# A two-part network on one core: the first part's second feed-forward product by seven block products instead of eight

## The reference

```python
x = x + jnp.concatenate([ya, yb, yc], axis=-1) @ w_out
u = _rms(x, norm2) @ w_ff1
return x + jnp.square(jax.nn.relu(u)) @ w_ff2
```

## Time and profile before

| | |
|---|---|
| runs | 2923.84, 2929.8, 2934.4 us; median 2929.8 us |
| span of the profiled execution | 2923.6 us |
| its TensorE clock granted, mean | 0.969 |
| PE busy | 2783.6 us (95%) |
| DVE busy | 1440.3 us (49%) |
| ACT busy | 988.4 us (34%) |
| POOL busy | 170.2 us (6%) |
| HBM read | 211.83 MB, 73 GB/s over the span |

### The profile page before, as it was taken

How to read it: one execution, slowest core, us unless ns; L and a number is a source line. 1 busy time by engine, 2 the same in 40 slices (tenths; PEclk the granted TensorE clock), 3 DMA queues, 4 the chain that set the end, 5 groups by cost and what they waited for, 6 DMA issues and landing times.

```text
span 2923.6 us, 45193 instructions
## 1 busy us (share of the span) xinstructions
PE 2783.6 (95%) x20028; PEld 2299.7 (79%) x20028; DVE 1440.3 (49%) x2242; ACT 988.4 (34%) x1490; POOL 170.2 (6%) x166
## 2 busy tenths in 40 slices
PE   8989999999989999999999799999999897999998
PEld 7877888878768888887768778888887587788887
DVE  4575533344475444433454574343634645743436
ACT  4344322233344232323342233232333522332422
POOL 0200000001100000000013300000000033000000
PEclk9998999999989999999989899999999898999999
DMA  5102222223003222221000033222220001132221
GB/s 192 50 1 97 87 101 96 92 73 114 17 8 136 94 94 101 93 92 52 15 1 30 20 128 115 90 102 90 85 73 29 1 3 46 73 130 101 87 101 58
DMA packets 31011, 216.83 MB, mean 74 GB/s; under 512 B 3680, under 2 KB 3936, under 8 KB 6368
## 3 DMA queue, kind: packets, MB, share of 16 engines
q1 hardware_dynamic: 30816, 213.94, 20.2%
HBM read 211.83 MB, written 2.10 MB: 73 GB/s over the span
## 4 chain that ended last, share of the span: by engine, by line
PE 88%; DVE 8%; ACT 2%; issue 1%; PEld 0%; PEldq 0%; DMA 0%; ACTq 0%; SPq 0%; DVEq 0%
PE PS L570 81%; PE PS L573 3%; PE PS L771 2%; DVE SC L1381 2%; DVE X L1389 1%; DVE R L1381 1%; DVE SM L1392 1%; PE PS L1185 1%; PE PS L1135 1%; DVE LN L1381 0%; PE PS L855 0%; DVE SM L1381 0%; ACT LN L2172 0%; PE PS L764 0%; PEld PS L570 0%
## 5 line engine op out<-in xcount | busy, mean ns | idle before, releaser
L570 PE MATMUL PS<-H,SPL 128*128 128x512 f32 (+1 forms) x4560 | 1054.2, 391 | 5.5 <-DVE H L1389 4.0
L570 PEld LDWEIGHTS PS<-H,SPL 128*128 128x128 f32 (+1 forms) x4560 | 851.5, 188 | 188.5 <-issue 7.0
L1381 DVE TENSOR_TENSOR SPL<-RAW,SPL 128x2048 fp32r<-128x2048 f32 (+3 forms) x192 | 429.6, 2239 | 680.5 <-ACT SPL L2172 677.5
L2172 ACT ACTIVATE SPL<-RAW 128x2048 fp32r<-128x2048 f32 (+3 forms) x192 | 358.0, 1868 | 783.0 <-PE PS L570 754.8
L570 PE MATMUL PS<-SPL,Uu 128*128 128x512 f32 x2592 | 589.8, 389 | 0.0
L570 PEld LDWEIGHTS PS<-SPL,Uu 128*128 128x128 f32 x2592 | 486.5, 188 | 101.0
L570 PE MATMUL PS<-SPL,H 128*128 128x512 f32 (+2 forms) x2016 | 432.1, 375 | 2.3 <-DVE SPL L1381 1.6
L570 PEld LDWEIGHTS PS<-SPL,H 128*128 128x128 f32 x2016 | 363.7, 189 | 69.2 <-DVE SPL L1381 2.1
L2172 ACT ACTIVATE R<-PS 128x512 f32<-128x512 f32 (+1 forms) x154 | 88.5, 584 | 187.0 <-PE PS L570 156.3
L1381 DVE TENSOR_TENSOR R<-R,PS 128x512 f32<-128x512 f32 (+1 forms) x98 | 64.8, 661 | 106.6 <-PE PS L570 91.2
L2172 ACT ACTIVATE Uu<-R 128x512 fp32r<-128x512 f32 x108 | 68.3, 632 | 142.2 <-DVE R L1381 142.2
(11 more groups left out here) (240 smaller groups left out, 2481.7 us busy)
## 6 DMA issues: line engine op xcount, KB each, us to landing
RAW<-in_wA SPq DMA_DIRECT2D x84, 1024.0 KB, 4.8
RAW<-in_wB SPq DMA_DIRECT2D x84, 1024.0 KB, 4.8
RAW<-in_wAo SPq DMA_DIRECT2D x8, 1024.0 KB, 4.8
RAW<-in_wBo SPq DMA_DIRECT2D x8, 1024.0 KB, 5.0
LN<-in_ln SPq DMA_DIRECT2D x4, 1024.0 KB, 6.6
P<-in_pB SPq DMA_DIRECT2D x2, 1920.0 KB, 9.1
RAW<-in_wBm SPq DMA_DIRECT2D x4, 704.0 KB, 4.0
X<-in_x SPq DMA_DIRECT2D x4, 512.0 KB, 5.6
```

The source lines that it names most:

```text
L570: return pe.matmul(out, l_, r_, start=start, stop=stop)
L1381: return v.tensor_tensor(out, a, b, o)
L2172: return a.activation(out, in_, f, scale=scale)
```

## The change

In the first-kind layers (`QUADS` has the parts 0 to 3 for the layers 0 and 1, and none for 2 and 3) the down product of each part is made by seven products of blocks in place of eight. The matrix of hidden values (512 tokens x 1024) is cut into A11, A12, A21, A22 (256 tokens x 512), the weights (1024 x 1024) into B11, B12, B21, B22 (512 x 512, each one group of the stream). The products are

- P1 = A11·B11, P2 = A12·B21, P5 = S1·T1, P3 = S4·B22, P6 = S2·T2, P7 = S3·T3, P4 = A22·T4, in this order;
- the sums of weights T1 = B11 + B12, T2 = T1 + B22, T3 = B12 + B22, T4 = B21 + T2;
- the sums of hidden values S3 = A11 - A21, S1 = A21 - A22, S2 = -A22 - S3, S4 = A12 + S2, by VectorE (`row_sum`).

Each has 24 multiplies (2 tiles of 128 tokens x 4 blocks x 3). P6 and P7 go on in the banks 0 and 1 of P1, P3 goes on in the banks 4 and 5 of P5; a product that goes on in a bank first waits until VectorE has added what stands there to x. The 16 additions to x have the numbers of `xadd`.

The weight sums are made by transfers that GpSimd issues, which add what they read to what lies in SBUF (`accum_op`). T3 is made as soon as its block is loaded; T1, T2 and T4 are a chain, since T1 and T2 lie where B11 lay, and each sum waits until the low part of what lay there before is made. Raw weights now have four places (`RAW`, `RW2`, and `LN`), and a group's place and what frees it come from `load_plan`.

The root of the norm can no longer be applied behind the product, since blocks of tokens are mixed; TensorE spreads the roots over the partitions once a layer (`spread_roots`, between the first two groups of the first up product), ScalarE copies them to `RB`, and VectorE makes relu(u)·root from PSUM, which ScalarE squares in place.

```diff
-GROUPS_A, GROUPS_B = 47, 50
+LOADS_A, LOADS_B = 47, 50
+QUADS = ((0, 1, 2, 3), (0, 1, 2, 3), (), ())
...
+            def spread_roots(l):
+
+                pe.wait_ge(s.nr, 8 * (l + 1))
+                bank_free(4)
+                for t in range(4):
+                    ins = mm(bank(4)[:, t * 128:(t + 1) * 128], rms[t][:, 1:2].to_broadcast([128, 128]), C("ident"))
+                ins.then_inc(s.gtr, 1)
+                free[4] = (s.rc, l + 1)
+
+            def quad(key):
+
+                base, ready = n["xadd"], n.get("ul", 0)
+                added_to = {("P6", 0): 1, ("P6", 1): 2, ("P3", 0): 5, ("P3", 1): 6, ("P7", 0): 9, ("P7", 1): 10}
+                for name in PRODUCTS:
...
+                    pe.wait_ge(s.lo, i + 1)
+                    pe.wait_ge(s.ul, ready + lows)
+                    goes_on = (name, 0) in added_to
+                    for b in range(2):
+                        if goes_on:
+                            pe.wait_ge(s.xadd, base + added_to[name, b])
+                        else:
+                            bank_free(PBANKS[name][b])
...
+                low_operand("A12", slice(2, 4))
+                row_sum("S1")
+                low_parts()
+                low_operand("S1")
+                add("P1", 0, 0, 0, True)
+                add("P1", 1, 1, 0, True)
+
+                row_sum("S2")
+                add("P2", 0, 0, 0)
+                low_operand("S2")
+                row_sum("S4")
+                low_parts()
+                add("P2", 1, 1, 0)
+
+                low_operand("S4")
+                add("P5", 0, 2, 1, True)
+                low_parts()
+                add("P5", 1, 3, 1, True)
+
+                add("P3", 0, 0, 1, True)
+                low_parts()
+                add("P3", 1, 1, 1, True)
+
+                low_operand("A22")
+                low_parts()
+                add("P6", 0, 0, 1, op=ALU.subtract)
+                ended(0)
+                add("P6", 1, 1, 1, op=ALU.subtract)
+                ended(1)
+
+                low_parts()
+                add("P7", 0, 2, 0, True)
+                add("P7", 0, 2, 1, op=ALU.subtract)
+                add("P7", 1, 3, 0, True)
+                add("P7", 1, 3, 1, op=ALU.subtract)
+
+                low_parts()
+                add("P4", 0, 2, 0)
+                ended(2)
+                add("P4", 1, 3, 0)
+                ended(3)
...
+                    def squared(q, b):
+                        v.wait_ge(s.mm, full_at[(l, "up", p, q), b])
+                        stt(RU[q][:, b], bank(sets[q][b]), 0.0, RB, ALU.max, ALU.mult).then_inc(s.fv, 1)
...
+                g.wait_ge(s.raw[held["B12"]], landed["B12"])
+                g.dma_start(B12, block("B22"), accum_op=ALU.add).then_inc(s.tx, 16)
+                g.wait_ge(s.lo, j + 1)
+                g.dma_start(B11, block("B12"), accum_op=ALU.add).then_inc(s.ty, 16)
+                g.wait_ge(s.lo, j + 3)
+                g.dma_start(B11, block("B22"), accum_op=ALU.add).then_inc(s.ty, 16)
+                g.wait_ge(s.lo, j + 2)
+                g.wait_ge(s.ty, summed["T2"][1])
+                g.dma_start(B21, B11, accum_op=ALU.add).then_inc(s.ty, 16)
...
-                if i >= 2:
-                    sp.wait_ge(s.lo, i - 1)
-                sp.dma_start(raw(i), src).then_inc(s.raw[i % 2], 16)
+                if freed is not None:
+                    sp.wait_ge(s.lo, freed)
+                sp.dma_start(raw_slots[where][:, 0:w], src).then_inc(s.raw[where], 16)
```

More of the change, by code:

```diff
@@ L142, in weight_stream, with split_widths @@
     return stream
-def first_group(l):
-    return l * GROUPS_A if l < 2 else 2 * GROUPS_A + (l - 2) * GROUPS_B
+def split_widths(stream):
+    widths = []
+    loads, splits, quads = load_plan()
+    at = 0
+    for l in range(4):
+        k = first_load(l)
+        for _ in range(INPUTS[l] + 4):
+            widths.append(stream[k][1])
+            k += 1
+        for p, n_up in enumerate(N_UP[l]):
+            for _ in range(n_up):
+                widths.append(stream[k][1])
+                k += 1
+            widths += [2048] * 7 if p in QUADS[l] else [stream[k + i][1] for i in range(N_DOWN)]
+            k += N_DOWN
+    return widths
 def split_plan():
@@ L1321, in tensor @@
                     for q in range(2):
[L1322 to L1329, removed]
+                        chunk((l, "up", p, q), 2, of_h2, "F", sets[q], freed=lambda b: (s.fv, n("fv")),
+                              between=(lambda: spread_roots(l)) if p == q == 0 else None)
+                    quad((l, "down", p))
             for l in range(2):
@@ L1440, in chunk, with paid, low_operand @@
                             evict(b)
+            def paid():
+                while at["owed"]:
+                    at["owed"] -= 1
+                    low_parts()
+            def low_operand(which, ks=slice(0, 4)):
+                i, a_ = OPERANDS[which]
+                hi, lo = operand(i)
+                v.wait_ge(s.uh, n("uh"))
+                ins = tt(four(lo)[:, ks], a_[:, ks], four(hi)[:, ks].bitcast(f32), ALU.subtract)
+                if ks.stop == 4:
+                    ins.then_inc(s.ul, 1)
+                    n("ul")
@@ L2191, in high_part @@
             def high_part(j):
-                w = stream[j][1]
-                a.wait_ge(s.raw[j % 2], 16 * (j // 2 + 1))
+                w = widths[j]
+                where, landed, summed = splits[j]
+                if summed is None:
+                    a.wait_ge(s.raw[where], landed)
+                else:
+                    chained, value = summed
+                    a.wait_ge(s.ty if chained else s.tx, value)
                 if slot_prev[j] is not None:
@@ L2732, in scalar @@
                         logs()
[L2733 removed]
+                    if four_sums:
+                        a.wait_ge(s.fbv, 22 * l + 8 * p + 8)
+                        quad((2 + l, "down", p))
+                    else:
+                        dense("ln" if p == 2 else None)
         def gpsimd(g):
@@ L2910, in sync @@
             sp.dma_start(PSM[:, 0:NPS], ap["psm"]).then_inc(s.psm, 16)
-            for i, (src, w) in enumerate(stream):
+            for i, (l_, k_, where, freed) in enumerate(loads):
+                src, w = stream[first_load(l_) + k_]
                 if i == 3:
```

386 lines of the change are left out of this document (329 added, 57 removed).

## The result

The changed kernel takes 2936.7 us (median of 20 runs, 2926.1 to 2948.2) where the kernel before takes 2924.5 (20 runs, 2913.1 to 2936.9): a ratio of 1.0042, 95% interval 1.0029 to 1.0055. It is slower by 0.4%; 0.5% faster was forecast.

What follows compares the result with a forecast made beforehand. TensorE, busy 95% of the span, was taken as the bound. Roots 2.1 and layer end 2.9 lost, down products 19.5 gained: -14.5, so 2929.8 - 14.5 = 2915.3 us, range 2908 to 2956.

Steps and rivals of the forecast that it cites:

- The weight sums: Step on GpSimd's adding transfers in the down products: the chain T2, T4 lands in time and costs nothing.
- D: Time from issue to landing of a GpSimd transfer that adds: put at 7.6 us, free up to 7.85.
- c: Delay of T4's landing when a plain load shares the transfer engines: 2.8 us.
- latest landing that costs nothing: T4's limit, 25.1 us after a down product's first multiply, when ScalarE's part of its split must start for P7.
- My own case: Weight sums with D at 7.6 us, inside the limit by 0.25, costing nothing; D up to 8.2 had chance 0.43.
- the bounds of D: For the adding transfer: from below a plain load's 4.8 us, from above two loads in a row, 9.6.
- P3's wait: In each down product TensorE waits for VectorE's additions of P5: 2.8 us, then another 0.2, together 3.0.
- three signs of being wrong: D over 8.75 us, TensorE waiting for anything in the up products, or the granted clock below 1.00 there.
- Rival (b): Down products: adding transfers T2 then T4 hold P7, deciding from D = 8.75; 2943.3 us at D 9.6; chance 0.32.
- Rival (c): Down products: waits make the granted clock fall, one product at half clock each, 5.44 us; 2959 us; chance 0.03.
- The roots' multiplies: Spreading the roots once a layer by TensorE: 1.05 us a layer, 2.1 us lost in two layers.
- The end of the first layer: Behind the last multiply a late weight split delays P4's additions: 3.8 us in place of 0.94, 2.9 lost once.

Runs made afterwards that it cites:

- e1_late_loads: Changed kernel, with SyncE holding the next part's first plain load until the sum T4 has landed; ratio 0.9933 to the kernel before.
- e6_late_and_adds: Changed kernel with the edits of e1_late_loads and e4_adds_behind together; ratio 0.9922 to the kernel before.
- e7_split_first: e6_late_and_adds, with ScalarE rounding the last weight group ahead of its two squares at the first layer's end; ratio 0.989 to the kernel before.
- e5_second_late: Changed kernel, with only the second plain load beside T4's transfer held until T4 has landed; ratio 1.006 to the kernel before.
- e3_filled_wait: Changed kernel, with twelve multiplies whose result nobody reads ahead of P7's wait in parts 0 to 2; ratio 0.999 to the kernel before.
- e4_adds_behind: Changed kernel, with VectorE's additions reordered: P5's first ahead of P1's and P2's, P6's ahead of T4's split; ratio 0.9893 to the kernel before.
- e2_copies: Changed kernel, with GpSimd's transfers only copying, the sums of weight blocks left out; ratio 0.9921 to the kernel before.
- e8_short_fill: Changed kernel, with four multiplies whose result nobody reads ahead of P7's wait in parts 0 to 2; ratio 1.003 to the kernel before.

## Why the prediction was wrong

**The step that failed** is the end of T4's chain in "The weight sums": "T4 is issued at once and lands at 6.6 + 2D, later by c", with c = 2.8. Counted from the first multiply of the second part's down product:

| | forecast | measured |
|---|---|---|
| T2 issued | 6.6 | 6.8 |
| T2 landed | 14.2 | 14.6 |
| T4 issued | 14.2 | 15.3 |
| T4 landed | 24.6 | 27.2 |
| latest landing that costs nothing | 25.1 | 24.4 (27.2 less the wait of 2.8) |

D itself was right within 0.4: 7.9 for T2 here, 8.0 in the median. The miss of 2.6 us is 0.2 at the issue, 0.25 in T2, 0.7 of GpSimd's between a landing and its next issue, which I had at nothing, and 1.4 in T4: the sharing load cost 4.3 and not 2.8, though alone T4 takes 7.5 and not 7.6. (Alone it took 6.9 to 9.1 us in the parts of e1_late_loads, e6_late_and_adds and e7_split_first, so what the sharing costs is known to about 1 us.) My own case had 0.5 us of room for all of it (0.25 per transfer), and the bounds of D held neither GpSimd's hand-over nor sharing that costs more than the load's own engine time. e1_late_loads and e5_second_late show the sharing by itself. The limit moved too, by 0.7, because P3's wait turned out shorter and P7 was due sooner. None of the prediction's three signs of being wrong came: D is not over 8.75, and in the up products TensorE waits for nothing and the clock is 1.00. And the 2936.7 us lie inside the stated range of 2908 to 2956, but not by its reasoning: the range was built from values of D, and D stayed in the forecast's own case.

**Rival (b) happened**, in the place it named: the chain of T2 and T4 holds P7, in the six down products in which another part follows. By its own rule D would have had to be 8.75. The chain's excess is as if D had been (27.2 - 6.6 - 2.8) / 2 = 8.9, so the threshold was passed by the hand-over and the sharing, with D below it. The waits before P7 come to 19.3 us in all. In the last part of the first layer only 48 KB are loaded beside T4, and P7 waits for nothing; in that of the second layer it is 704 KB, and P7 waits 0.8 us. The forecast had a sharing load of 1 MB in all eight.

**Rival (c) came with it**, after P7's wait and not P3's: 1.8 to 3.1 us in each of six products, some 12.5 in all (this is what is left of their length without the waits and 38.3 us of multiplies; about 0.3 of each is there without a fall too, as in the product of e5_second_late above), against the 5.4 per wait with which it was priced at a chance of 0.03. Without it the rest would have come out about even, as e3_filled_wait's 0.999 shows. Both were listed as alternatives, and they add up.

**P3's wait** was forecast at 2.8 + 0.2 and is 1.7, with no second one: 8 x 1.3 = 10.4 us to the good. Most of the reason is in VectorE's timeline: operations that follow one another without a wait overlap by up to 0.1 us.

```profile
428.95 1.22 DVE L1554 TENSOR_TENSOR R<-R,RU 128x1024 f32<-128x1024 f32 x1
430.22 2.29 DVE L1554 TENSOR_TENSOR SPL<-RW,SPL 128x2048 fp32r<-128x2048 f32 x1
432.43 1.22 DVE L1554 TENSOR_TENSOR Uu<-R,Uu 128x1024 fp32r<-128x1024 f32 x1
433.56 1.28 DVE L1554 TENSOR_TENSOR X<-X,PS 128x512 f32<-128x512 f32 x2
434.76 1.22 DVE L1562 SCALAR_TENSOR_TENSOR R<-RU,R 128x1024 f32<-128x1024 f32 x1
```

The split of 2.29 is followed after 2.21, the operand of 1.22 after 1.13. The list added full durations: P5's first addition ends at 19.0 in it and at 18.1 in the trace (443.44 + 0.68 less 426.05), which is 0.9 of the 1.1 us by which the first wait is shorter. VectorE is busy for 34.5 us of a down product, not 37, and the same overlaps, counted once each, fit that.

**Small parts.** The roots' multiplies took 1.05 us a layer, as forecast. The end of the first layer was forecast at 2.9 lost. From the last multiply to the next product's first it was 4.8 us before (from the start of the turning in the earlier trace rows to 650.18), 8.8 in the changed kernel (642.85 to 651.65) and 7.1 in e1_late_loads: 4.0 lost, of which 1.7 because 25 turnings took 4.62 us, at a granted clock of 0.63, where they take 2.95 at 1.00 in e1_late_loads, behind waits of the same length; why it fell in the one and not in the other no run shows. Without that fall the loss is 2.3, so the forecast's 2.9 was near for the mechanism it named, the late weight split; e7_split_first takes 2.7 us of what e6_late_and_adds has there back.

**The sum** in the profiled executions: the 168 multiplies take 38.3 us and not 38.1, so they give back 41.5 and not 43.5. Then -41.5 of multiplies, +32.8 of waits, +12.8 behind the waits before P7, +2.1 of roots and +4.0 at the layer's end make +10.2. The two feed-forward stretches, from the first multiply of the first up product to the first of the next layer's input product, are longer by 5.5 us in the first layer (353.2 before, 358.7 after) and by 4.4 in the second (353.0 and 357.4), 9.9 together. So the account closes there. The two spans differ by 5.6 and the medians by 12.2, since the other stages vary by as much or more from run to run: from the first product of the third layer to the end it is 1641.8 us in the trace before, 1639.6 in the one after, and 1635 to 1649 in the experiments.

The page "DMA: Bandwidth & Descriptors" of the Trainium skill (Specifications) had GpSimd's first byte 0.4 us later than SyncE's, and an estimated D of 8.0 by it; the traces are near it (D is 8.0, and a copy takes 5.1 against the plain load's 4.8). By that rule the forecast would still have lacked the sharing and the hand-over.

**A version that beats both.** e4_adds_behind (0.9893) and e7_split_first (0.989) are about 1.1% faster than the kernel before. There a down product is 43.5 - 38.3 = 5.2 us shorter, nearly all of the 5.44 that 24 multiplies fewer are worth, once nothing that TensorE needs stands behind T4's split or S4's.

## What to carry to other kernels

When a product is made of fewer multiplies and more additions, list for each late operand what stands behind its preparation in an in-order engine: T4 was needed 32.7 us in, and held TensorE at 29 through two additions that had nothing to do with it. Where two transfers follow one another by a semaphore, count the hand-over, and let a transfer that shares the engines cost more than its neighbour's own time. Where a forecast has a wait of some 2 us or more in a dense stream of multiplies, put what runs behind it at half clock into the price of that wait; here it came behind 15 of 16 such waits.

## What the runs showed of the hardware

- A transfer of 1 MB that adds to its target in SBUF takes 8.0 us from a source in HBM, 6.9 to 9.1 from one in SBUF, median 7.0 in e1_late_loads and 7.4 in e6_late_and_adds and e7_split_first, when no plain load shares the engines; as a copy 5.1 and 4.4 to 4.7 (e2_copies). Beside one plain load of 1 MB the second kind takes 11.7 (e5_second_late), beside one of 704 KB 9.1 (changed kernel).
- GpSimd is busy 0.88 us with the issue of one that adds, 0.53 with a copy's, and issues 0.7 us after the landing for which it waited.
- Ahead of P7 TensorE waited 1.9 to 3.5 us in 16 down products of the changed kernel, e5_second_late and e8_short_fill. In 15 of them the granted clock fell behind the wait, to 0.55 to 0.63 over the windows shown, near the 1.2 GHz level, and once, behind 2.79 us, it stayed at 1.00. It stayed there too behind all 48 waits of 1.7 us at P3 and behind P7's waits of 0.4 to 1.6. With the wait of 2.8 filled by multiplies whose result nobody reads, the clock stayed. What decides between waits of 1.7 and 1.9, and what spared the one of 2.79, no run shows.
- Operations of VectorE's that follow one another without a wait overlap by up to 0.1 us: 2.21 us from start to start where the first lasts 2.29.
